# An encoder trunk on one core: the order of softmaxes, conv norm and loads in the pooling part, and the statistics of the last output block

## What is computed

```python
def mixer(x, mem, w_in, conv_w, ..., w_out):
    h = x @ w_in
    a = a_val * jax.nn.sigmoid(a_gate)
    a = causal_depthwise_conv(a, conv_w, conv_b)                # width 31, 384 channels
    a = jax.nn.silu(layer_norm(a, conv_ln_g, conv_ln_b))
    p = pool_mixer(p_in, pool_w, pool_scale)                    # trailing means of 2, 4, 8, 16; 384 channels
    mo = memory_cross_attention(q, mem, w_mk, w_mv)             # 4 heads, 256 memory tokens
    return jnp.concatenate([a, p, mo], axis=-1) @ w_out
```

## Time and profile before

| | us |
|---|---|
| median of 3 runs | 1965.62 |
| lowest, highest | 1964.35, 1966.64 |
| the profiled execution, its own time | 1968.15 |
| its span | 1966.4 |
| TensorE busy in the span | 1877.1 (95%) |
| VectorE, ScalarE, GpSimd busy | 1475.7, 940.2, 218.0 |

### The profile page before, as it was taken

One profiled execution on the slowest core, in us unless ns is written; L12 is line 12 of the kernel. 1 busy time (PEld: TensorE's weight loads), 2 busy tenths in 40 slices (PEclk: granted clock), 3 DMA queues, 4 the chain that ended last, 5 costly groups with the idle time before them and its releaser, 6 DMA issues.

```text
span 1966.4 us, 26236 instructions
## 1 busy us (share of the span) xinstructions
PE 1877.1 (95%) x8722; PEld 1562.3 (79%) x8722; DVE 1475.7 (75%) x1926; ACT 940.2 (48%) x1598; POOL 218.0 (11%) x311
## 2 busy tenths in 40 slices
PE   5999999689999899999999999999999998999997
PEld 5788889568888688888888788888887786887786
DVE  6544238669887988888888988877778768557898
ACT  2211115645665556565566756555557335225231
POOL 1111013100000211212220021000000000000111
PEclk9999999989999999999999999999999999999999
DMA  6422225544544733333435342221215668458443
GB/s 224 168 105 70 71 84 192 169 152 141 174 149 168 256 129 137 141 139 128 149 122 198 129 147 101 94 85 75 85 75 172 219 220 283 170 171 278 172 159 120
DMA packets 171787, 296.13 MB, mean 151 GB/s; under 512 B 11712, under 2 KB 106176, under 8 KB 171712
## 3 DMA queue, kind: packets, MB, share of 16 engines
q1 hardware_dynamic: 171712, 295.18, 43.2%
HBM read 189.23 MB, written 105.91 MB: 150 GB/s over the span
## 4 chain that ended last, share of the span: by engine, by line
PE 68%; DVE 9%; DMA 4%; ACT 2%; issue 2%; SPq 0%; POOL 0%; DVEq 0%; ACTq 0%; POOLq 0%
PE banks L2191 55%; PE banks L1102 7%; DVE mov_lo L2396 2%; DMA y_scratch<-up_and_out 2%; DVE sta_lo L2392 1%; PE banks L1136 1%; DMA mov_raw<-in_w_down 1%; PE banks L1035 1%; PE banks L1084 1%; PE banks L1055 1%; PE banks L1117 1%; ACT mov_hi L2260 1%; DVE up_and_out L2430 1%; DVE up_and_out L2427 1%; PE banks L1066 1%
## 5 line engine op out<-in xcount | busy, mean ns | idle before, releaser
L2191 PE MATMUL banks<-mov_hi,sta_hi 128*128 128x512 f32 x1848 | 725.1, 392 | 25.2 <-DVE mov_lo L2396 9.0
L2191 PE MATMUL banks<-mov_lo,sta_hi 128*128 128x512 f32 x1848 | 722.1, 391 | 0.0
L2191 PE MATMUL banks<-mov_hi,sta_lo 128*128 128x512 f32 x1848 | 721.7, 391 | 0.0
L2191 PEld LDWEIGHTS banks<-mov_hi,sta_hi 128*128 128x128 f32 x1848 | 348.7, 189 | 107.2 <-issue 16.6
L2191 PEld LDWEIGHTS banks<-mov_hi,sta_lo 128*128 128x128 f32 x1848 | 348.8, 189 | 73.0
L2191 PEld LDWEIGHTS banks<-mov_lo,sta_hi 128*128 128x128 f32 x1848 | 349.0, 189 | 72.1
L2253 ACT ACTIVATE sta_hi<-sta_raw 128x512 fp32r<-128x512 f32 (+1 forms) x340 | 198.5, 611 | 147.7 <-PE banks L2191 100.6
L2392 DVE TENSOR_TENSOR sta_lo<-sta_raw,sta_hi 128x512 fp32r<-128x512 f32 (+1 forms) x340 | 223.5, 673 | 40.6 <-ACT sta_hi L2253 38.6
L279 PE MATMUL banks<-x0t_hi,win_hi 128*128 128x512 f32 x320 | 126.5, 395 | 1.6 <-DVE x0t_lo L401 1.6
L2282 ACT ACTIVATE half_sums<-banks 128x512 f32<-128x512 f32 x68 | 40.7, 598 | 179.0 <-PE banks L2191 179.0
L279 PE MATMUL banks<-x0t_hi,win_lo 128*128 128x512 f32 x320 | 124.8, 390 | 0.0
(11 more groups left out here) (239 smaller groups left out, 2710.7 us busy)
## 6 DMA issues: line engine op xcount, KB each, us to landing
sta_raw<-in_w_up SPq DMA_DIRECT2D x88, 512.0 KB, 4.1
hidden_scratch<-up_and_out SPq DMA_DIRECT2D x44, 512.0 KB, 2.6
y_scratch<-up_and_out SPq DMA_DIRECT2D x16, 1024.0 KB, 7.8
sta_raw<-hidden_scratch SPq DMA_DIRECT2D x32, 512.0 KB, 4.5
up_and_out<-y_scratch SPq DMA_DIRECT2D x16, 1024.0 KB, 4.9
x_operands<-x_operands_out SPq DMA_DIRECT2D x56, 256.0 KB, 4.3
mov_raw<-x_operands SPq DMA_DIRECT2D x14, 1024.0 KB, 7.5
mov_raw<-in_w_down SPq DMA_DIRECT2D x44, 256.0 KB, 4.6
```

The costliest lines, as they stand in the source:

```text
L2191: last = pe.matmul(psum, w, x, start=(start and k == 0 and i == 0), stop=(stop and k == m - 1 and i == 2), skip_group_check=True)
```

## The change

It moves steps between the turns of the pair loop on all four engines and changes the end of the last block. Apart from waits, no instruction of the mixing part is added or removed.

- Chunk 0: maxima(0,0) one turn sooner; scores(0,1) from turn 11 to turn 9, before the second fold; its exps and scalings to turn 10. turn(0,0), turn(0,1) and attend(0) a turn sooner.
- Chunk 1: scores(1,0) from turn 16 to 11, scores(1,1) from 18 to 17; exps(1,0) from 17 to 14.
- Conv norm of chunk 0: conv_total from turn 17 to 14, mean 17 to 16, deviations 18 to 16, variance 21 to 20, deviation and scaling 22 to 20, swish 23 to 22, which puts it ahead of pair 23's evacuation on ScalarE.
- attend(1) and mean(1) leave the loop and stand inside project_first, between the attention rows and the pooled rows. TensorE's wait for conv_lo of chunk 0 now stands ahead of all of this.
- w_out rows 6 and 7 are raised after the last pair; rows 3, 4 and 5 are loaded and raised sooner.
- SyncE loads pairs 15 to 23 up to two turns sooner; chunk 1's pooled rows are loaded behind x0 and the constants of LayerNorm 1; VectorE's wait for these constants moves from ahead of residual(0,0) to ahead of affine(0,0).
- Last block: two of the four `bn_stats` come before the last two additions, tile 0's last pass comes before tile 1's centring, tile 1's last pass and its store are done in two halves of 512 columns.

```diff
@@ -840,7 +840,7 @@
             for m in range(NP):
-                if m + 4 < NP:
+                if m < last_conv - 1:
                     load_pair(sp, m + 4)
@@ -866,24 +866,30 @@
                     load_wo(2)
+                if m == last_conv - 1:
+                    load_pair(sp, m + 4)
+                    load_pair(sp, m + 5)
                 if m:
                     store_pair(m - 1)
+                if m == last_conv:
+                    load_pair(sp, m + 5)
+                if last_conv <= m < NP - 6:
+                    load_pair(sp, m + 6)
+                if m == last_conv:
+                    load_wo(3)
+                    load_wo(4)
                 if m == last_conv + 1:
...
                     load_chunk(sp, 1, 1, 0, CT, land[1])
-                if m == last_conv + 2:
-                    load_wo(3)
-                    load_wo(4)
-                if m in (17, 18, 20):
-                    load_wo({17: 5, 18: 6, 20: 7}[m])
+                if m in (14, 17, 19):
+                    load_wo({14: 5, 17: 6, 19: 7}[m])
             store_pair(NP - 1)
...
             load_chunk(sp, 0, 0, CT, 2 * CT, mc_loaded[0])
-            load_chunk(sp, 1, 1, CT, 2 * CT, mc_loaded[1])
             sp.wait_ge(bands_hi, len(POOL_WINDOWS))
@@ -891,6 +897,7 @@
             sp.dma_start(g_b[:, 1, :], a["ln1_b"].rearrange("(o n) -> o n", o=1).to_broadcast((P, D))).then_inc(consts, 16)
+            load_chunk(sp, 1, 1, CT, 2 * CT, mc_loaded[1])
@@ -1102,21 +1109,15 @@
-            def project_first():
-
-                tok, pooled = slice(0, P), range(CT, 2 * CT)
-                pe.wait_ge(o_lo, 1)
-                pe.wait_ge(c_lo, 1)
-                for ks in ([k for k in range(KT) if k not in pooled], pooled):
-                    if ks is pooled:
-                        pe.wait_ge(p_l, 1)
-                    for b in range(2):
-                        cols = slice(b * 512, (b + 1) * 512)
-                        for k in ks:
-                            for i, (w, x) in enumerate(exact_parts(mx_hi[0][:, k, tok], mx_lo[0][:, k, tok], wo_hi[:, k, cols], wo_lo[:, k, cols])):
-                                last = pe.matmul(ps_y[:, b, :], w, x, start=(k == 0 and i == 0), stop=(k == 2 * CT - 1 and i == 2))
-                        if ks is pooled:
-                            last.then_inc(y_ready, 1)
+            def project_first(ks):
+
+                for b in range(2):
+                    cols = slice(b * 512, (b + 1) * 512)
+                    for k in ks:
+                        for i, (w, x) in enumerate(exact_parts(mx_hi[0][:, k, 0:P], mx_lo[0][:, k, 0:P], wo_hi[:, k, cols], wo_lo[:, k, cols])):
+                            last = pe.matmul(ps_y[:, b, :], w, x, start=(k == 0 and i == 0), stop=(k == 2 * CT - 1 and i == 2))
+                    if 2 * CT - 1 in ks:
+                        last.then_inc(y_ready, 1)
@@ -1193,33 +1194,28 @@
                     fold(0)
+                    scores(0, 1)
                 if m == 10:
...
                 if m == 11:
-                    scores(0, 1)
-                if m == 13:
+                    scores(1, 0)
+                if m == 12:
                     pe.wait_ge(ident_ok, 3)
...
                     turn(0, 0)
-                if m == 15:
+                if m == 14:
                     turn(0, 1)
                 if m == 16:
-                    scores(1, 0)
-                if m == 17:
                     attend(0)
                     mean(0)
+                if m == 17:
+                    scores(1, 1)
                 if m == 18:
-                    scores(1, 1)
-                if m == 19:
                     turn(1, 0)
+                if m == 20:
+                    variance(0)
                 if m == 21:
                     turn(1, 1)
-                    variance(0)
-                if m == 23:
-                    pe.wait_ge(o_lo, 1)
-                    attend(1)
-                    pe.wait_ge(c_std, 1)
-                    mean(1)
@@ -1245,8 +1241,17 @@
+            pe.wait_ge(c_lo, 1)
+            pe.wait_ge(wo_l, 2 * CT)
+            project_first(range(CT))
+            pe.wait_ge(o_lo, 1)
             pe.wait_ge(wo_l, KT)
-            project_first()
+            project_first(range(2 * CT, KT))
+            attend(1)
+            pe.wait_ge(c_std, 1)
+            mean(1)
+            pe.wait_ge(p_l, 1)
+            project_first(range(CT, 2 * CT))
             variance(1)
@@ -1410,43 +1415,41 @@
                 if m == 9:
+                    exps(0, 0)
                     fold_out(0)
-                    exps(0, 0)
                 if m == 10:
+                    exps(0, 1)
+                    query_hi(1, 1)
                     fold_out(1)
+                if m == 11:
+                    wout_hi(3)
                 if m == 12:
-                    exps(0, 1)
-                if m == 13:
-                    query_hi(1, 1)
+                    turned_hi(0, 0)
                 if m == 14:
-                    turned_hi(0, 0)
+                    turned_hi(0, 1)
+                    exps(1, 0)
                 if m == 15:
-                    wout_hi(3)
+                    wout_hi(4)
                 if m == 16:
-                    turned_hi(0, 1)
-                    wout_hi(4)
+                    attn_hi(0, 0)
                 if m == 17:
-                    exps(1, 0)
+                    squares(0, 0)
+                    wout_hi(5)
                 if m == 18:
-                    attn_hi(0, 0)
-                    wout_hi(5)
-                if m == 19:
-                    squares(0, 0)
                     exps(1, 1)
+                    turned_hi(1, 0)
                 if m == 20:
-                    turned_hi(1, 0)
-                    wout_hi(6)
+                    deviation(0)
                 if m == 21:
-                    wout_hi(7)
+                    turned_hi(1, 1)
                 if m == 22:
-                    turned_hi(1, 1)
-                    deviation(0)
-                if m == 23:
                     act.wait_ge(land[0], 48)
                     swish(0, 0)
+            wout_hi(6)
+            wout_hi(7)
+            pooled_hi(0, 0)
             attn_hi(1, 1)
             squares(1, 1)
-            pooled_hi(0, 0)
@@ -1477,8 +1480,8 @@
+            deviation(1)
             query_hi(2, 0)
-            deviation(1)
             norm(0, 0)
@@ -1696,52 +1699,49 @@
                     wout_lo(2)
+                    maxima(0, 0)
+                if m == 9:
                     edge_ratios()
-                if m == 9:
-                    maxima(0, 0)
+                    normalise(0, 0)
                     fold_low(0)
+                    maxima(0, 1)
                 if m == 10:
-                    normalise(0, 0)
-                    fold_low(1)
-                if m == 12:
-                    maxima(0, 1)
-                if m == 13:
                     normalise(0, 1)
                     query_low(1, 1)
+                    fold_low(1)
+                if m == 11:
+                    maxima(1, 0)
+                    wout_lo(3)
+                if m == 12:
+                    turned_lo(0, 0)
+                if m == 14:
+                    turned_lo(0, 1)
+                    normalise(1, 0)
+                    conv_total(0, 0)
                 if m == 15:
-                    wout_lo(3)
-                if m == 14:
-                    turned_lo(0, 0)
+                    wout_lo(4)
                 if m == 16:
-                    turned_lo(0, 1)
-                    wout_lo(4)
+                    attn_lo(0, 0)
+                    deviations(0, 0)
                 if m == 17:
-                    conv_total(0, 0)
-                    maxima(1, 0)
+                    maxima(1, 1)
+                    square_sum(0)
+                    wout_lo(5)
                 if m == 18:
-                    deviations(0, 0)
-                    normalise(1, 0)
-                    attn_lo(0, 0)
-                    wout_lo(5)
-                if m == 19:
-                    maxima(1, 1)
-                if m == 20:
-                    square_sum(0)
                     normalise(1, 1)
                     turned_lo(1, 0)
-                    wout_lo(6)
+                if m == 20:
+                    conv_total(1, 1)
+                    scale_conv(0, 0)
                 if m == 21:
-                    conv_total(1, 1)
-                    wout_lo(7)
-                if m == 22:
                     turned_lo(1, 1)
-                    scale_conv(0, 0)
             dve.wait_ge(g_mm, NG)
             conv_lo(0, 0)
+            wout_lo(6)
+            wout_lo(7)
+            pooled_lo(0, 0)
             attn_lo(1, 1)
             deviations(1, 1)
-            pooled_lo(0, 0)
-            dve.wait_ge(consts, 32)
@@ -1775,12 +1775,13 @@
+            square_sum(1)
             residual(0, 0)
-            square_sum(1)
-            query_lo(2, 0)
             residual(0, 1)
...
```

(62 more changed lines are left out.)

## The result

The changed kernel takes 1945.95 us (median of 6 runs, 1944.66 to 1946.82) against 1964.03 for the kernel before beside it (6 runs, 1963.11 to 1966.64): a ratio of 0.9903 [0.9894, 0.9913], which is 19.0 us less (17.1 to 20.8); the two medians by themselves lie 18.1 apart. A second set of 4 runs gave 1946.41 and 0.9903 [0.9886, 0.9920]. The profiled execution: own time 1944.67, span 1943.0. The forecast was 1950: right in sign and place, 4 us too high, with the result near the lower end of its range.

A forecast was written before the change was run, and what follows sets the result against it. Bound by the order in VectorE's and ScalarE's in-order queues in the pooling part. 17.0 - 0.4 - 2.0 + 1.1 = 15.7 us takes the median from 1965.6 to 1950, range 1945.5 to 1957.5.

The forecast's parts named there:

- What bounds it: Pooling part, pairs 12 to 23: order in VectorE's and ScalarE's queues, not arithmetic, leaves TensorE 23.3 us idle.
- Part 4: Last block: statistics moved earlier and last pass halved give 0.95 us, the smaller last store 0.15; sum 1.1 us.
- Part 1: Pooling part: softmaxes earlier, laid out by hand from measured durations; project_first starts at 390.4 against 410.9.
- Part 2: project_first: attend(1) and mean(1) inside cost 3.5 us in full, slow start kept; it ends 17.0 us sooner.
- The residual's 0.4 us: Behind project_first: project(0,0,2) waits 0.4 us for residual(0,0), queued on VectorE behind chunk 1's tail.
- Part 3: SyncE's queue: earlier pair loads, later conv chunk load costed at nothing, moved consts wait nothing, chunk 2's load landing about 408.
- The rule on small transfers: Last store: the skill's advice to coalesce speaks against halving; its fixed-cost split would save about 0.6 us, an estimate.
- A hand schedule takes every handover at its best: Pooling part: 2.0 us set against the gain, an estimate of about 20 handovers at 0.1 us more.
- (a): Pairs 358 to 385: their own pace binds, TensorE stays slow; gain 8 to 11 us, time 1955 to 1958, chance 0.2.
- (c): Pooling part: softmaxes come early but conv norm keeps its date; gain 1 to 3.5 us, chance 0.04.
- (d): Pooling part: late chunk loads stop VectorE at conv_total(0,0) and the pairs; slower, above 1970, chance 0.03.
- (b): Pooling part and products: no slow start, no handover loss; gain 20 to 21 us, time 1945, chance 0.08.

The follow-up runs named there:

- x11: The kernel before with only attend(1) and mean(1) moved amid the first products, chunk 1's rest ordered as in the changed kernel: 1968.27 us, ratio 1.0011.
- x9: The changed kernel with 12 extra, unused matmuls after pair 23, in TensorE's wait for the first w_out products: 1942.16 us beside 1966.08 for before.
- x3: The changed kernel with attend(1) and mean(1) put back after pair 23, ahead of the wait for chunk 0's conv_lo: 1945.82 us.
- x8: The changed kernel with attend(1) and mean(1) after pair 23 and chunk 0's swish behind pair 23's evacuation: 1940.14 us, ratio 0.9867.
- x6: The changed kernel with the pool pairs' loads at their old turns, w_out rows at their new ones: 1949.85 us, ratio 0.9915.
- x5: The kernel before with only chunk 0's conv norm one or two turns sooner, swish ahead of pair 23's evacuation: 1963.41 us, ratio 0.9989.
- x1: The kernel before with only the new end of the last block (statistics, last passes, stores): 1963.64 us beside 1964.98, ratio 0.9995.
- x10: The changed kernel with the second tile's centring again ahead of the first tile's last pass: 1945.99 us, a single execution.
- x13: The changed kernel itself run once more; no time of its own is given, its first product came 51.5 us after fold(0).

## Why the forecast was right, and where it was wrong

- **What bounds it.** Right. The stretch was bound by order in two in-order queues; the same work in another order took 18 us less, and the rows behind moved as a block, as said. Of the signs named, TensorE's idle up to the first product was 8.1 us, where 12 were forecast; no matmul waited for the pooled rows, as said; the last normalise came 0.5 us closer to the last matmul, where 0.9 were forecast (Part 4).
- **Part 1, the hand schedule.** Right to within 1 us over 50. From fold(0), the first product was forecast at 390.4 - 337.9 = 52.5 and came at 51.6. Pair 21's wait: 2.5 forecast, 2.2 in the trace; the wait for probT_lo: 1.1 and 1.1; conv sum: 367.7 to 368.5 forecast, 366.6 to 367.4 in a span that ran 0.8 ahead.
- **Part 2.** Right in sum: 17.0 from the first product to the end, 16.9 measured (16.0 to 17.4 over four executions). It is 3.5 for attend(1) and the slow start, both as said; x11 prices the first, x9 shows the second. The pooled rows were ready at 397.9, wanted at 400.5, so not late. That the place in the idle was free to be kept (x3, x8) I didn't see: I took the 4 to 5 us of idle as given and asked only whether the move gains.
- **The residual's 0.4 us.** Not there: project(0,0,2) followed variance(1) without a wait.
- **Part 3.** Half right. Chunk loads: no wait at conv_total, landing 3.3 to 4.8 us after issue, and chunk 2's load had landed by 408.4 where I said 408. But I read the new turns of the pair loads only for what they might cost. They are worth 3.7 us (x6), which the hand schedule held without my saying so, since it never let ScalarE wait for a load. The moved wait for consts was worth nothing in the changed kernel, as said, since its constants landed in time; in x5, where they didn't, the old place cost, and that I hadn't considered.
- **Part 4.** Right in sum, by luck: 1.1 forecast, 1.2 measured, 1.0 by the times of x1. Its two terms missed in opposite directions. VectorE's passes were put at 0.95 and gave 0.5, because the last one waits 0.51 us for GpSimd; with the old order of the two passes (x10) they gave 0.9. The smaller store was put at 0.15 and gave 0.7. The step that the swap of normalise and scaling gains nothing was thus wrong by some 0.3 us (x10).
- **The rule on small transfers.** The forecast read the Trainium skill (DMA: Bandwidth & Descriptors, Rules for kernel authors) as speaking against the halved store. That rule is on many small transfers and names 64 KB as the size under which overhead rules; the halves have 256. The trace sides with halving: the last store, of 256 KB, landed in 2.0 us, against 2.6 to 2.8 for the two of 512 KB. So it saves some 0.6 to 0.8, near the 0.6 that the forecast worked out from the Trainium skill's Anatomy of one DMA (same page). Only the difference agrees: that split was fitted to DMAs issued by GpSimd, and its 2.0 us fixed plus bytes would give an estimate of 2.6 us for 256 KB, where these stores, issued by SyncE, took 2.0.
- **The sum: the step that failed.** "A hand schedule takes every handover at its best", 2.0 us set against it. It was an allowance without a row. With VectorE and ScalarE 91% busy from 356 to 378, more than the 80% I feared, the handovers cost nothing beyond the 0.1 us already in the schedule, and the start came 0.9 sooner even than the schedule without the allowance. Of the 3.5 us between forecast (71.9 from fold(0) to project(0,0,2), all terms in) and measurement (68.4), 2.0 is this allowance, 0.9 the start, 0.4 the residual, 0.1 to 0.2 the products; the end adds 0.1. The rest up to 4 us is within the scatter of medians.
- **The rivals.** (a) fell: the clock of the pairs was 1.00 in 356 to 378, against 0.84, and low only in the last 6.5 us (0.74), and there not in every execution (1.00 in x13 and x10). The idle spells ahead of the pairs are shorter, 2.2 us at the most in place of 6.8; that this is what kept the clock up is likely, but no run varied it by itself. (c) fell, the conv norm's end came 21 us sooner; (d) fell with the landings above. (b)'s time of 1945 is the nearest, but for another reason than it gave: the slow start stayed, the loss at handovers did not.

The two things to do better were thus small: take a term of the sum only from rows, and after a hand schedule ask for each remaining idle spell what could lie in it.

## What to carry to other kernels

Where two in-order queues release a third engine, lay the schedule out by hand from measured durations and take its sum: here it was right to 1 us in 50, and the allowance on top of it was the error. Read a change as a whole: the loads alone gave 0 us, the conv norm alone 2, all but the conv norm 11, the whole 19, and a wait that was covered before became the limit when only half was done. When an idle spell of TensorE can't be removed, put work into it that is due anyway: it saves its own time and the slow start behind it.
